# Two Strassen-like products of an MLP with a new order of work, ScalarE and GpSimd reading the whole first chain

## What is computed

```python
x = x + o @ w_o
u = jax.nn.relu(_rmsnorm(x, g_mlp) @ w_up)
return x + (u * u) @ w_down
```

## Time and profile before

| | us |
|---|---|
| median of three runs | 3713.87 |
| profiled execution, its own time | 3703.22 |
| its span in the profile | 3701.6 |
| TensorE busy | 3330.0 (90%) |
| GpSimd busy | 2133.7 (58%) |
| VectorE busy | 1752.1 (47%) |
| ScalarE busy | 1464.2 (40%) |
| `mlp_up`, from the first matmul to the last GpSimd instruction | about 2163 to 2908 |
| `mlp_down`, from the first DMA issue to the end | 2912 to 3701.6 |

### The profile page before, as it was taken

The page is one execution under the profiler, slowest core; times in us unless marked ns, Lnnn a source line. Parts: engine busy times, 40 slices in busy tenths (PEclk is TensorE's granted clock), DMA queues, the critical chain, the costliest instruction groups (busy, mean ns, idle before and its releaser), DMA issues. The chain is left out here.

```text
span 3701.6 us, 50940 instructions
## 1 busy us (share of the span) xinstructions
PE 3330.0 (90%) x17168; PEld 2483.8 (67%) x17168; DVE 1752.1 (47%) x2876; ACT 1464.2 (40%) x2333; POOL 2133.7 (58%) x1687
## 2 busy tenths in 40 slices
PE   7999999799997999799979969998999688898898
PEld 7987788555555666545438857776777466676666
DVE  2223323465636666243323354445444466666665
ACT  3323222255553666422222243334333344444444
POOL 1223456477774666302322257776776588877776
PEclk9999999899999999899989989999999899999999
DMA  5546767866664776689866735445443533343333
GB/s 196 193 161 211 228 197 218 217 172 196 192 177 130 194 194 173 237 306 323 312 189 198 270 91 153 129 140 192 128 128 117 185 118 123 125 165 144 121 128 132
DMA packets 466664, 666.72 MB, mean 180 GB/s; under 512 B 55122, under 2 KB 343380, under 8 KB 459220
## 3 DMA queue, kind: packets, MB, share of 16 engines
q1 hardware_dynamic: 429428, 528.64, 46.0%
q10 hardware_dynamic: 23032, 80.04, 6.3%
q0 software_dynamic: 13952, 54.80, 4.1%
HBM read 483.15 MB, written 247.86 MB: 197 GB/s over the span
## 5 line engine op out<-in xcount | busy, mean ns | idle before, releaser
L3406 POOL TENSOR_TENSOR down_acc<-fox_in_squares,down_acc 128x512 f32<-128x512 f32 x256 | 433.4, 1704 | 115.9 <-ACT fox_in_squares L3368 112.2
L3499 PE MATMUL down_c<-down_w_hi,down_u_hi 128*128 128x512 f32 x808 | 329.4, 408 | 77.5 <-ACT fox_in_squares L3368 75.2
L3500 PE MATMUL down_c<-down_w_lo,down_u_hi 128*128 128x512 f32 x808 | 324.1, 401 | 0.0
L3501 PE MATMUL down_c<-down_w_hi,down_u_lo 128*128 128x512 f32 x808 | 322.9, 400 | 0.0
L3163 PE MATMUL up_c<-up_h_hi,up_w_hi 128*128 128x512 f32 x672 | 269.0, 400 | 58.0 <-DVE up_u L3115 56.2
L681 PE MATMUL proj_z<-proj_w_lo,proj_x_hi 128*128 128x512 f32 (+1 forms) x816 | 304.4, 373 | 0.0
L680 PE MATMUL proj_z<-proj_w_hi,proj_x_hi 128*128 128x512 f32 (+1 forms) x748 | 281.3, 376 | 10.7 <-DVE proj_w_lo L519 10.7
L682 PE MATMUL proj_z<-proj_w_hi,proj_x_lo 128*128 128x512 f32 (+1 forms) x748 | 276.1, 369 | 0.0
L3368 ACT ACTIVATE fox_in_squares<-down_c 128x512 f32<-128x512 f32 x256 | 152.7, 596 | 309.5 <-PE down_c L3501 293.9
L3165 PE MATMUL up_c<-fin_h_h_lo,up_w_hi 128*128 128x512 f32 x672 | 264.2, 393 | 0.0
L3166 PE MATMUL up_c<-up_h_hi,up_w_lo 128*128 128x512 f32 x672 | 264.2, 393 | 0.0
(11 more groups left out here) (344 smaller groups left out, 8599.9 us busy)
## 6 DMA issues: line engine op xcount, KB each, us to landing
down_u_lo<-scratch_uc SPq DMA_DIRECT2D x64, 896.0 KB, 6.2
samp_v_in<-in_cache_v POOLq DMA_DIRECT2D x128, 256.0 KB, 4.9
fin_wr<-in_w_up SPq DMA_DIRECT2D x64, 512.0 KB, 5.0
scratch_uc<-up_su SPq DMA_DIRECT2D x128, 256.0 KB, 4.5
fin_wr<-in_w_down SPq DMA_DIRECT2D x16, 2048.0 KB, 7.9
out_new_win_k<-in_win_k ACTq DMA_DIRECT2D x8, 4080.0 KB
out_new_win_v<-in_win_v ACTq DMA_DIRECT2D x8, 4080.0 KB
scratch_uc<-up_u SPq DMA_DIRECT2D x96, 256.0 KB, 5.6
```

The costliest lines, as they stand in the source:

```text
L3406: pool.tensor_tensor(to, out[(4 * m + ACT_READS[k] - 1) % 2], to, ALU.add).then_inc(pool_added, 1)
L3499: pe.matmul(bank, hi, w1, start=(cc == 0 and k in (1, 5, 2)), stop=False, skip_group_check=True)
L3500: pe.matmul(bank, hi, w2, start=False, stop=False, skip_group_check=True)
L3501: mm = pe.matmul(bank, lo, w1, start=False, stop=(cc == 1 and k in (4, 3, 2)), skip_group_check=True)
```

## The change

`join_heads` writes the blocks `hc` in the order `UP` = 1, 6, 5, 7, 2, 4, 3 and is otherwise untouched.

In `mlp_up` the products go in the order `UP`, and product 1 of the next step goes ahead of product 3 of this one. Between k = 7 (whose read VectorE makes from chain 1) and k = 3 (which continues chain 1) there are now three products. The relus on ScalarE and the squares on GpSimd are gone: VectorE does both in one instruction for three quarters (`scalar_tensor_tensor`, max with 0, then times itself) and multiplies the fourth quarter's PSUM bank by ScalarE's relu of it. The factors h are split in halves, have one more buffer (`NP + 1`), and those of group 1 are loaded one product earlier, some of them ahead of the stores of the su blocks. At its end `mlp_up` already loads the first block of w_down.

In `mlp_down` all 16 tiles of the result stay in `acc`, so each of the eight blocks of w_down is loaded and split once. Two units go in step: 32 steps of 14 products in the order of the table `SLOTS` (k, side). ScalarE still copies every read of chain 0, eight per step, and GpSimd adds them; VectorE adds six. The factors u come per half step in two loads (4 and 3 entries), and on SyncE's queue a block of w_down is issued behind a load of u instead of ahead of it. The samples' product accumulates over q in one PSUM bank and is added once. The last unit's result is stored in four quarters.

```diff
+UP = (1, 6, 5, 7, 2, 4, 3)
...
-    seq = [(n, k) for n in range(STEPS_N) for k in ORDER]
-    H_LAG = 3
+    seq = [(0, 1)] + [(n, k) for n in range(STEPS_N) for k in UP[1:6]] + [(STEPS_N - 1, 3)]
+    for n in range(STEPS_N - 1, 0, -1):
+        seq[1 + 5 * n:1 + 5 * n] = [(n, 1), (n - 1, 3)]
...
-            def relu(n, q):
-                act.wait_ge(read_dve, 3 * n + RELUS[q])
-                act.activation(u[:, q, :], u[:, q, :], ACT.Relu).then_inc(relu_done, 1)
...
-                pool.tensor_tensor(u[:, q, :], u[:, q, :], u[:, q, :], ALU.mult).then_inc(sq_done, 1)
...
+                if k == 4:
+                    dve.wait_ge(read_act, 4 * n + 4)
+                    dve.tensor_tensor(u[:, q, :], c_ps[0][n % 2][:, :], u[:, q, :], ALU.mult).then_inc(sq_done, 1)
+                if k in DVE_READS:
+                    dve.wait_ge(read_dve, 3 * n + DVE_READS[k])
+                    dve.scalar_tensor_tensor(u[:, q, :], u[:, q, :], 0.0, u[:, q, :], ALU.max, ALU.mult)\
+                        .then_inc(sq_done, 1)
...
+            load_w_down(sp, dram, wr, wd_loaded, 0)
+            store_block(STEPS_N - 1)
...
-    Q_N = N_GROUPS_T * KBLOCKS
-    UNITS = Q_N * UNITS_Q
-    RING = NP + 4
+    SLOTS = ((1, 0), (5, 0), (1, 1), (5, 1), (6, 0), (6, 1), (2, 0), (7, 0), (3, 0), (7, 1), (4, 0), (3, 1), (4, 1), (2, 1))
...
+    UNITS = N_GROUPS_T * PAIRS_T
+    STEPS_Q = UNITS // 2
+    STEPS = KBLOCKS * STEPS_Q
+    RING = NP + 1
...
+    FILLS = {(2, 9): 0, (3, 3): 1, (3, 6): 2, (3, 9): 3, (3, 12): 4, (0, 2): 5, (0, 5): 6}
...
-        acc = ph.sb("acc", [P, 2 * PAIRS_T, D_MODEL])
+        acc = ph.sb("acc", [P, 2 * UNITS, D_MODEL])
...
+                if h + 2 < 2 * STEPS:
+                    sp.wait_ge(product, NP * h)
+                    load_u(h + 2)
+                if (p, half) == (0, 1) and q + 1 < KBLOCKS:
+                    sp.wait_ge(w_split, NP * q + 6)
+                    sp.wait_ge(t_made, 4 * (q + 1))
+                    sp.wait_ge(s_done, q + 1)
+                    load_w_down(sp, dram, wr, wd_loaded, q + 1)
...
+                        if n >= 2:
+                            act.wait_ge(pool_added, n - 1)
+                        act.activation(out[n % 2], c_ps[0][SLOTS[s][1]][:, :], ACT.Copy).then_inc(read_act, 1)
...
+                    which = {(1, 3): 0, (1, 5): 1, (3, 3): 2, (3, 5): 3}.get((p, at))
+                    if which is not None and q + 1 < KBLOCKS:
+                        make_t(q + 1, which)
```

More of the change, by code:

```diff
@@ L2921, in sampled, with turning @@
             return BLOCKS <= n < STEPS_N
+        def turning(e):
+            for back, half in ((4, 1), (3, 0)):
+                if e > back and seq[e - 1 - back][0] == BLOCKS - 1:
+                    yield seq[e - 1 - back][1], half
         @block.sync
@@ L3066, in _ @@
                 make_s(0, which)
-            for which in range(4):
+            for which in range(3):
                 make_s(1, which)
             for n in range(STEPS_N):
-                more = n + 2 < STEPS_N
-                if more:
+                if n > 0:
+                    make_su(n - 1)
+                if n + 1 < STEPS_N:
+                    make_s(n + 1, 3)
+                if n + 2 < STEPS_N:
                     make_s(n + 2, 0)
@@ new lines, in entries, with u_place, part @@
+        def entries(half, side):
+            count = 4 - half if side == 0 else 3 + half
+            first = 0 if side == 0 else 4 - half
+            return first, count
+        def u_place(k, side, half):
+            first, count = entries(half, side)
+            at = POS[k] - (0 if half == 0 else 4 if side == 0 else 3)
+            assert 0 <= at < count
+            return first + at
+        def part(h, side):
+            first, count = entries(h % 2, side)
+            return u_hi[h % U_SLOTS][:, first:first + count, :, :], u_lo[h % U_SLOTS][:, first:first + count, :, :]
@@ new lines, in _ @@
+            last = STEPS - 1
+            for s in (6, 8, 7, 10):
+                was_added(sp, last, s)
+            store_unit(last, 0)
+            unit = UNITS - 1
+            for s in (9, 11, 12, 13):
+                was_added(sp, last, s)
+                i, j = QUARTERS[SLOTS[s][0]]
+                sp.dma_start(dram["y"][(2 * unit + i) * P:(2 * unit + i + 1) * P, j * D_G:(j + 1) * D_G], quarter(last, s))\
+                    .then_inc(y_sent, 16)
+            sp.wait_ge(y_sent, 16 * (UNITS + 3))
@@ new lines, in _ @@
+            for j in range(2, NP):
+                lo_w(0, j)
+            for w in range(STEPS):
+                for s, (k, side) in enumerate(SLOTS):
+                    if s in by_dve:
+                        dve.wait_ge(product, N_SLOTS * w + s + 1)
+                        quarter_free(dve, w, s)
+                        to = quarter(w, s)
+                        dve.tensor_tensor(to, c_ps[CHAIN[k]][side][:, :], to, ALU.add).then_inc(dve_added, 1)
+                    h = 2 * w + s // NP + 1
+                    if s % NP in (2, 5) and h < 2 * STEPS:
+                        lo_u(h, s % NP // 5)
+                    fill = fill_at(w, s - 1)
+                    if fill:
+                        lo_w(*fill)
+                if w == STEPS - STEPS_Q:
+                    dve.wait_ge(s_done, KBLOCKS)
+                    dve.wait_ge(xs_loaded, 32)
+                    dve.tensor_tensor(acc_s[:, :], s_ps[:, :], acc_s[:, :], ALU.add).then_inc(s_added, 1)
```

555 lines of the change are left out of this document (250 added, 305 removed).

## The result

| | before | changed |
|---|---|---|
| median of four runs each, us | 3710.13 (3700.04 to 3715.04) | 3518.80 (3510.39 to 3522.88) |
| profiled execution, us | 3703.22 | 3519.46 |
| TensorE busy | 3330.0 (90%) | 3289.1 (94%) |
| GpSimd busy | 2133.7 (58%) | 1890.7 (54%) |
| VectorE busy | 1752.1 (47%) | 1762.3 (50%) |

The account below looks back on a forecast made before the run. TensorE, 88 to 90% busy in both MLP products, was taken as close to the bound, its waits the question. 3703.2 less 64 (mlp_up) and 112 (mlp_down) gave 3527, plus half of 10.7 for the median: 3532 us, range 3498 to 3600.

Parts of the forecast that it names:

- turnaround: In mlp_up, three products between 7 and 3 remove the gap before product 3: 29 x 1.72 = 50 us gone.
- VectorE's added work: In mlp_up, three relu-squares of 1.1 us and a multiply per step: VectorE takes 13.6 us in 19.25, hidden.
- Change of the row group: In mlp_up, earlier loads and half factors shorten the two long gaps: 12 us saved, bounds 0 and 20.
- Start of `mlp_down`: w_down is already there: first product 7.5 us in instead of 14.5, plus 3 us for the low clock at first.
- Backlog of loads: In mlp_down, 8 MB of x1 queued ahead of the fourth load of u cost 4 us, bounds 0 and 12.
- Stall of the pair: In mlp_down, GpSimd and VectorE work that cannot overlap stalls TensorE, chiefly in fourth steps: 17 us, between 0 and 37.
- 43.7 us without a gap: Argument against the first rival: before, TensorE ran 43.7 us gapless in a q of mlp_down whose pair was full.
- rival 1: GpSimd and VectorE together bound mlp_down: 37 us of stall instead of 17, 3552 us, or 3562 with low clock; chance 0.15.
- Gap of 4.2 us per q: In mlp_down, TensorE's gap, put down to u queued behind 2 MB of w_down, should go with u issued first.
- 2: Rival: VectorE becomes the bound in mlp_up at 20.6 us per step, 43 us more, 3575 us; chance 0.07.
- 3: Rival: mlp_up's turnaround gap only moves, for example to product 6; 50 us less gain, 3582 us; chance 0.04.
- 4: Rival: loads of u come too late in mlp_down, a gap per half step costs 365 us, about 3890; chance 0.03.

Follow-up runs that it names:

- e5: Changed kernel, but in mlp_down VectorE reads the bank after product 4 from PSUM, so GpSimd has six adds per step instead of eight: 3504.59 us (0.9445).
- e3: Changed kernel with relus back on ScalarE and squares back on GpSimd, new order of products kept: 3522.72 us (0.9515).
- e7: Changed kernel without the interleaving: product 1 of the next step no longer goes ahead of product 3: 3553.31 us (0.9583).
- e9: e5 with the samples' square in mlp_up on ScalarE instead of GpSimd: 3506.35 us (0.9451).
- e6: Changed kernel with the first samples' product of mlp_down moved behind the seventh slot instead of ahead of everything: 3525.07 us (0.9507).
- e8: Changed kernel with the w_down load issued ahead of the load of u on SyncE's queue again: 3518.15 us (0.9489).
- e4: Changed kernel with GpSimd's adds in mlp_down covering 8 of the 512 columns only (result not the product): 3506.09 us (0.9451).
- e10: e8 with SyncE first waiting for five more products, so w_down goes ahead of u and both are issued late: 3536.25 us (0.9532).
- e11: Changed kernel with the wait for five more products on SyncE, u still issued ahead of w_down: 3520.98 us (0.95).

## Why the prediction was right, point by point

- **Cost of a matmul, steps.** 0.229 us and 19.25 per step were forecast; e5's q gives (80.39 - 3.65) / 336 = 0.2284, a step of 19.2 in `mlp_down`, and in `mlp_up` a step takes 19.13. From that, 32 steps of `mlp_down` are 614 us instead of 616.
- **`mlp_up`, turnaround: 50 us.** Held: all 29 gaps are gone. e3 and e7 show that the order, with its interleaving, is the whole cause. The size was 29 x 1.82 = 53, since the prediction priced a gap at 1.72.
- **VectorE's added work: hidden.** Held. 1.1 us were taken for a relu-and-square, 1.08 is the mean. In the step shown above VectorE is busy for 12.9 us, where 13.6 were forecast.
- **Change of the row group: 12, bounds 0 and 20.** The gaps fell from 8.00 + 8.34 to 5.51, 10.8 us, and the time lost at the lower clock level there from 4.5 to 1.7: 13.6. The prediction took off 3.1 us for two usual gaps that it counted in no other term. That VectorE's splits would still bound it was half right: in e9 a split releases TensorE, but behind 5.3 us in which VectorE waited for GpSimd.
- **Start of `mlp_up`: 2.** Measured 3.7: 4.1 us from its first DMA issue to the first product instead of 6.7, and 1.1 behind that, 0.4 of gaps and 0.7 at the lower clock level. Its end, not counted, is 1.8 us shorter. In all 53 + 13.6 + 3.7 + 1.8 = 72.1 us came where 64 stood.
- **Start of `mlp_down`: 7.5 + 3.** Measured 12.0 to the first product, which then runs at full clock. "The eighth is issued while TensorE waits for u" was wrong in size: the samples start 5.5 us after the first issue, when their own load has landed, and take 6.55 us at the lower level, while u is ready after 6.9 (e6). e6's profile, 4.7 us longer, speaks for their place all the same.
- **Backlog of loads: 4.** It costs nothing: ScalarE waits for u 4.1 us in the whole stage, and TensorE doesn't. It is there, though: with w_down ahead of u, e8 has its only long wait for u (6.75 us) in the first q.
- **Stall of the pair: 17.** Measured 7 x 1.8 = 12.6, and e4 and e5 show that it is the pair. The 17 was a choice between 0 and 37 by an argument, so that it came within 4.4 us is in part luck. Place and form were off. I had the stall in the fourth step; it falls in the first step of the next q, in two pieces. That the two `out` buffers and ScalarE's slack carry the debt so far is my reading of the waits, not shown by a run. The copy waiting for GpSimd was forecast as releaser, the weight split on VectorE was not. The arithmetic that gave 77.6 us for a q of 80.7 was right in its verdict: it fits, but not evenly. By its own terms, 24.5 in a step of 19.25, 5.2 us of debt arise and 1.8 reach TensorE.
- **"43.7 us without a gap" before.** This argument against rival 1 was read from the second row group alone. In six q of the first group TensorE has three more gaps besides the long one, 1.6 to 2.2 us in all, and the first of them goes back to the same wait for GpSimd:

```profile
3016.55 0.60 ACT L3368 ACTIVATE fox_in_squares<-down_c 128x512 f32<-128x512 f32 x1 [1.06 <-POOL down_acc L3406]
...
3017.29 0.47 PE L3499 MATMUL down_c<-down_w_hi,down_u_hi 128*128 128x512 f32 x1 [0.67 <-ACT fox_in_squares L3368]
```

So the pair already cost TensorE something before, and the rival deserved more than it got. The long gap, too, was read at its short end: it is 4.2 to 6.0 us over the stage, not 4.21 to 4.27. Neither reading went into the sum.
- **Gap of 4.2 us per q: gone.** It is, but my reason was half of it, and that the whole gap went was luck. It was worth much: the gap stood 14 times in the stage before, 66.8 us in all. "Queued behind 2 MB of w_down" named the order on the queue; e8 shows that the order alone costs nothing behind the first q, and e10 and e11 that the load of u must be late as well. The change had removed both.
- **End: 4.5.** Measured 6.3 from the last matmul's record (3511.4) to the end of the span.
- **Sum.** `mlp_down`: 12.0 + 614 + 25.5 + 12.6 + 6.3 = 670.4, against 670.6 in the profile and 677.5 forecast. The 5 us added for the median did not come: the median lies 0.7 below its own profiled execution. Both stages gave 15 us more than forecast, the 5 us for the median came on top, and the stages ahead took 7 back by chance, so 13 us remain between 3532 and 3519.
- **Rivals.** 1 falls: no stall of 5 us, no low clock. 2 falls: VectorE 67% busy in a step. 3 falls for the changed kernel, and e7 shows its mechanism one edit away, at 32 x (20.18 - 19.13) = 34 us instead of 50. 4 falls.

On the rule of the Trainium skill (SBUF — State Buffer, "Who interferes with whom"), that the later of the two instructions is blocked for the whole of the other: VectorE's 10 us less per q in e4 agree with it, and the sum of 7.96 us goes further, since it was held up for a row of seven instructions and not for one. The first rival, built on it, failed by its size: the pair did stall TensorE, but for 1.8 us per q and not for 5.
